# Output projection in four pieces, a third of w_mod moved from VectorE to TensorE, rows spread through DRAM, one multiplication moved to GpSimd

## What is computed

```python
mod_x = silu(c) @ w_mod + b_mod                 # w_mod is 1024 x 6144; six rows of 1024:
x_sh1, x_sc1, x_g1, x_sh2, x_sc2, x_g2 = split(mod_x, 6)
ux = modulate(rmsnorm(x), x_sh1, x_sc1) @ w_in  # the same for the context
pool_x = pool_mixer(ux[:, :512])                # windows 2/4/8/16, then w_pool
ssm_x = ssm_output(scan both ways of ux[:, 512:])  # 32 groups, 64 complex states; then GELU, w_glu
x = x + x_g1 * (concat([pool_x, ssm_x]) @ w_out)
h2 = modulate(rmsnorm(x), x_sh2, x_sc2)
x = x + x_g2 * moe(h2)                          # 32 experts, top 2, each 3 matrices of 2 MB
return rmsnorm(x)
```

## Time and profile before

| | |
|---|---|
| median of 3 runs | 686.17 us (685.89 to 686.75) |
| the profiled execution's own time | 685.61 us |
| its span, first to last instruction | 683.8 us |
| TensorE busy (matmuls) | 596.1 us, 87% |
| VectorE, ScalarE, GpSimd busy | 207.4, 147.6, 35.7 us |
| moved by DMA | 247.27 MB, 362 GB/s over the span |

### The profile page before, as it was taken

How to read it: one execution, slowest core, us unless ns; L and a number is a source line. 1 busy time by engine, 2 the same in 40 slices (tenths; PEclk the granted TensorE clock), 3 DMA queues, 4 the chain that set the end, 5 groups by cost and what they waited for, 6 DMA issues and landing times.

```text
span 683.8 us, 9370 instructions
## 1 busy us (share of the span) xinstructions
PE 596.1 (87%) x3784; PEld 253.1 (37%) x3784; DVE 207.4 (30%) x432; ACT 147.6 (22%) x235; POOL 35.7 (5%) x84
## 2 busy tenths in 40 slices
PE   1878999869878999789889978988997898899995
PEld 0345463446434334234323423422342342234331
DVE  7987979538663002001000200100020010002003
ACT  7163051022112212110301211130121213011111
POOL 4364000000000000000000000000000000000000
PEclk9999999988979999999989999998999999899999
DMA  8992177899866999999999999999999999998951
GB/s 319 417 391 66 30 260 292 302 372 404 335 256 263 424 422 420 422 422 422 422 422 422 421 422 422 422 422 422 422 422 422 422 422 422 422 422 342 422 230 62
DMA packets 45807, 247.27 MB, mean 362 GB/s; under 512 B 8548, under 2 KB 11252, under 8 KB 18520
## 3 DMA queue, kind: packets, MB, share of 16 engines
q1 hardware_dynamic: 41032, 244.45, 87.9%
q10 hardware_dynamic: 4448, 1.57, 0.9%
q0 software_dynamic: 304, 0.93, 0.4%
HBM read 242.75 MB, written 2.10 MB: 358 GB/s over the span
## 4 chain that ended last, share of the span: by engine, by line
PE 64%; DMA 21%; DVE 3%; issue 2%; ACT 2%; SPq 1%; ACTq 0%; POOL 0%; DVEq 0%; POOLq 0%
DMA wts<-in_w_up 21%; PE ps L784 20%; PE ps L819 16%; PE ps L758 5%; PE ps L540 4%; PE ps L752 4%; PE ps L549 2%; PE ps L617 2%; PE ps L666 1%; PE ps L677 1%; PE ps L795 1%; PE ps L463 1%; DVE ra L1070 1%; PE ps L647 1%; PE ps L566 1%
## 5 line engine op out<-in xcount | busy, mean ns | idle before, releaser
L784 PE MATMUL ps<-wts,ra 128*64 128x512 f32 x512 | 240.1, 624 | 37.3 <-DMA wts<-in_w_up 36.1
L785 PE MATMUL ps<-wts,ra 128*64 128x512 f32 x512 | 240.2, 624 | 0.0
L784 PEld LDWEIGHTS ps<-wts,ra 128*64 128x64 f32 x512 | 70.5, 143 | 186.5 <-issue 137.2
L819 PE MATMUL ps<-rc,ra 128*32 128x512 f32 x512 | 111.4, 593 | 0.0
L819 PE MATMUL ps<-wts,ra 128*32 128x512 f32 x512 | 111.4, 593 | 0.0
L1070 DVE TENSOR_TENSOR ra<-ra,ps 128x256 f32<-128x256 f32 x32 | 13.5, 421 | 297.7 <-ACT ra L1023 297.5
L1017 ACT COPY ra<-ps 128x512 f32<-128x512 f32 x32 | 33.6, 1049 | 232.5 <-PE ps L785 232.5
L785 PEld LDWEIGHTS ps<-wts,ra 128*64 128x64 f32 x512 | 70.5, 143 | 0.0
L819 PEld LDWEIGHTS ps<-wts,ra 128*32 128x32 f32 x512 | 29.1, 110 | 73.2 <-issue 73.2
L1070 DVE TENSOR_TENSOR cb<-ps,ra 128x512 f32<-128x512 f32 x32 | 22.1, 692 | 103.4 <-PE ps L819 103.4
L1012 ACT COPY ra<-ps 128x512 f32<-128x512 f32 x32 | 18.5, 588 | 114.5 <-PE ps L752 108.6
(11 more groups left out here) (228 smaller groups left out, 507.4 us busy)
## 6 DMA issues: line engine op xcount, KB each, us to landing
wts<-in_w_up SPq DMA_DIRECT2D x64, 1024.0 KB, 15.3
wts<-in_w_gate SPq DMA_DIRECT2D x64, 1024.0 KB, 13.2
wts<-in_w_down SPq DMA_DIRECT2D x30, 1024.0 KB, 9.4
rc<-in_w_down SPq DMA_DIRECT2D x30, 1024.0 KB, 12.5
wts<-in_w_mod SPq DMA_DIRECT2D x15, 1024.0 KB, 13.1
r<-in_w_mod SPq DMA_DIRECT2D x7, 1024.0 KB, 7.3
wts<-in_w_in SPq DMA_DIRECT2D x2, 2048.0 KB, 23.0
wts<-in_w_out SPq DMA_DIRECT2D x2, 2048.0 KB, 11.6
```

The source lines that it names most:

```text
L784: pe.matmul(ps[0:64, 4 + b, :], st, Wg[b][:, k, :], start=(k == 0), stop=(k == KD - 1))
L785: mm = pe.matmul(ps[64:128, 4 + b, :], st, Wu[b][:, k, :], start=(k == 0), stop=(k == KD - 1))
L819: mm = pe.matmul(ps[32 * j:32 * j + 32, BANKS[n], :], hid[:, j, f, SLOTS * t:SLOTS * t + SLOTS], Wd[j][:, f, 512 * h:512 * h + 512], start ...
```

## The change

- **Last third of w_mod.** `mod_sum` and `acc` are gone. TensorE takes the 8 pieces as it takes the others (4 matmuls each, PSUM bank 7), between pieces of other work. The pieces go to four buffers (`wm2`).
- **Rows through DRAM.** The rows of the bias and of the products stay in `modrow`. ScalarE writes them to the DRAM tensor `row_dram` with a DMA, and `sp` reads each back with a DMA that gives it to all 128 partitions: `gffb` (0.5 MB), `g1b` and `sh2b` (1 MB together), `sc2b` (0.5 MB), `g2b` (0.5 MB). VectorE makes `A2b` of `sc2b` and `gffb` in one instruction. `spread`, lines 684, 690, 734 and 735 and ScalarE's four copies are gone.
- **mix_pool in four pieces** of 4 matmuls, among the pieces of w_mod and the parts of `y` and GLU. The Toeplitz part of `y` comes ahead of them.
- **Toeplitz kernels** go to `wts`, where `ST` was, and their 15 DMAs are issued ahead of the loads of w_mod blocks 6 and 7 and no longer wait for the input projection.
- **Half of the second direction's `MO`** (6 of VectorE's instructions of 128x1024) goes to GpSimd, and VectorE waits for it (`mo_back`) ahead of its scan.
- **Transposes of SA**: those of the first direction's second half come after the last w_mod block of third 0, those of the second direction between the matmuls of `u_ssm(1)`. VectorE copies three of the sets.
- **First loads of the experts**: up of expert 0 and down of expert 1 among the last w_mod blocks; down of expert 0 after `mix_pool`.
- **gather in two halves**: gathers 0 and 1 ahead of `gate_up(i, 0)`, 2 and 3 after its k = 3.

```diff
@@ SyncE
             sp.wait_ge(S("s_mm"), 8)
-            sp.dma_start(wpool, w_pool[0].rearrange("g c d -> c g d")).then_inc(S("wpool_in"), 16)
             sp.dma_start(wo_pool, w_out_v[:, 0:4, :]).then_inc(S("wo_pool_in"), 16)
-            for k in range(6, KD):
-                mod_chunk(1, k)
-
-            sp.wait_ge(S("u_pool_mm"), NT)
-
             sp.wait_ge(S("kt_ready"), 2)
             for t in range(L):
...
+            for k in range(6, KD):
+                mod_chunk(1, k)
+
+            sp.wait_ge(S("u_pool_mm"), NT)
+            sp.dma_start(wpool, w_pool[0].rearrange("g c d -> c g d")).then_inc(S("wpool_in"), 16)
             sp.dma_start(wglu, w_glu[0].rearrange("(k p) n -> p k n", p=P)).then_inc(S("wglu_in"), 16)
             sp.dma_start(wo_ssm, w_out_v[:, 4:8, :]).then_inc(S("wo_ssm_in"), 16)
             for k in range(3):
                 mod_chunk(2, k)
...
-            sp.wait_ge(S("mix_pool"), 1)
+            sp.wait_ge(S("gff_row"), 16)
+            sp.dma_start(gffb, row_dram[1:2, 0:D].broadcast_to([P, D])).then_inc(S("gff_in"), 16)
+            sp.wait_ge(S("mod1_row"), 16)
+            sp.dma_start(ra[:, 6144:8192], row_dram[0:1].broadcast_to([P, 2048])).then_inc(S("g1_in"), 16)
+            sp.wait_ge(S("pool_mm"), 1)
+            mod_chunk(2, 3)
+
             sp.wait_ge(S("hp_ready"), 1)
+            mod_chunk(2, 4)
             sp.wait_ge(S("y_mm"), 1)
             for t in range(NT):
                 sp.dma_start(x2[:, t, :], x[0, t * P:(t + 1) * P]).then_inc(S(f"xres_in{t}"), 16)
+            mod_chunk(2, 5)
             gu_load(sp, 0, 0, 0, "up")
             gu_load(sp, 0, 0, 1, "up")
-            for k in range(6, KD):
-                mod_chunk(2, k)
+            mod_chunk(2, 6)
             for half in range(2):
-                down_load(sp, lambda j: j, half, (0, 1))
-            sp.wait_ge(S("mod2_used"), KD)
+                down_load(sp, lambda j: j, half, (1,))
+            mod_chunk(2, 7)
+            sp.wait_ge(S("mix_pool"), 1)
+            for half in range(2):
+                down_load(sp, lambda j: j, half, (0,))
+            sp.wait_ge(S("mod2_row"), 16)
+            sp.wait_ge(S("hp_ready"), 1)
+            sp.dma_start(sc2b, row_dram[2:3, 0:D].broadcast_to([P, D])).then_inc(S("sc2_in"), 16)
             gu_load(sp, 0, 0, 0, "gate")
@@ GpSimd
+            gp.wait_ge(S("kk_mm"), 2)
+            gp.wait_ge(S("sa_t"), 16)
...
+            for h in range(2):
...
+                gp.tensor_tensor(MOv[:, 1, 0, g], pr, cr, ALU.mult)
+                step(gp.tensor_tensor(t, pi, ci, ALU.mult))
+                step(gp.tensor_tensor(MOv[:, 1, 0, g], MOv[:, 1, 0, g], t, ALU.subtract))
+            gp.sem_inc(S("mo_back"), 1)
@@ TensorE
+            mix_pool(0)
+            for k in range(3):
+                mod_chunk(2, k, 7)
 
             pe.wait_ge(S("hp_ready"), 1)
...
+            for k in range(6, KD):
+                mod_chunk(2, k, 7)
+            mix_pool(3).then_inc(S("mix_pool"), 1)
             pe.wait_ge(S("wo_ssm_in"), 16)
@@ TensorE, gate_up
                     if j == 0 and k == 0:
-                        pe.wait_ge(S("xm_ready"), 4 * i + 3)
-                    if j == 0 and k == 6:
-                        pe.wait_ge(S("xm_ready"), 4 * i + 4)
+                        pe.wait_ge(S("out_copy"), 4 * i + 3)
+                    if j == 0 and k % 2 == 0:
+                        pe.wait_ge(S("xm_ready"), 4 * i + k // 2 + 1)
...
+                    if j == 0 and k == 3:
+                        pe.wait_ge(S("out_copy"), 4 * i + 4)
+                        gather(2)
+                        gather(3)
@@ VectorE
+            dve.wait_ge(S("sc2_in"), 16)
+            dve.wait_ge(S("gff_in"), 16)
+            link(dve.scalar_tensor_tensor(A2b.rearrange("p (k q) -> p k q", k=KD), sc2b.rearrange("p (k q) -> p k q", k=KD), 1.0,
+                                          gffb.rearrange("p (q k) -> p k q", k=KD), ALU.add, ALU.mult))
```

More of the change, by code:

```diff
@@ L160, in hybrid_block @@
         sg = rc[:, 3072:4096].rearrange("p (q t c) -> p q t c", q=4, t=L)
-        g1b = cb[:, 3072:4096]
+        g1b = ra[:, 6144:7168]
+        sh2b = ra[:, 7168:8192]
+        gffb = ra[:, 4096:5120]
+        sc2b = cb[:, 0:1024]
         g2b = ra[:, 6656:7680]
         gfb = r2[:, 0:1024]
-        A2 = aux[:, 16:24]
-        A2b = rc[:, 1024:2048]
-        sh2b = rc[:, 4096:5120]
-        A2diag = rc[:, 2048:3072]
+        A2b = rc[:, 0:1024]
         x2 = rc[:, 6144:8192].rearrange("p (t d) -> p t d", t=NT)
@@ L610, in _ @@
             mm.then_inc(S("pool_mm"), 1)
-            pe.wait_ge(S("wo_pool_in"), 16)
-            pe.wait_ge(S("cat_pool"), 1)
-            for n in range(4):
-                for k in range(4):
-                    mm = pe.matmul(ps[:, n, :], cat[:, k, P * (n // 2):P * (n // 2) + P],
-                                   wo_pool[:, k, 512 * (n % 2):512 * (n % 2) + 512], start=(k == 0), stop=False)
-            mm.then_inc(S("mix_pool"), 1)
             pe.wait_ge(S("toep_in"), 16 * (2 * L - 1))
@@ L651, in _ @@
             mm.then_inc(S("y_mm"), 1)
[L652 to L653 removed]
+            mod_chunk(2, 3, 7)
+            mix_pool(1)
             pe.wait_ge(S("ysb_ready"), 1)
@@ L658, in _ @@
             mm.then_inc(S("y_t"), 1)
+            for k in range(4, 6):
+                mod_chunk(2, k, 7)
+            mix_pool(2)
             pe.wait_ge(S("wglu_in"), 16)
@@ L943, in _ @@
             u_evacuate(0)
+            for n in range(8, 2 * KD):
+                copy_st(n)
             u_evacuate(1)
-            copy_st(1, 0)
-            copy_st(1, 1)
             u_evacuate(2)
@@ L1043, in _ @@
                 four(i)
-                for r in range(4):
+                for r in range(2):
                     take_gathered(4 * i + 4, r)
@@ L1144, in _, with powers_times @@
             dve.sem_inc(S("bbar_ready"), 1)
-            def powers_times(dst, pw, m, d, sign_im, done):
-                    for rr in range(2):
+            def powers_times(dst, pw, m, d, sign_im, done, rs=(0, 1), between=None):
+                    for rr in rs:
+                        if between and rr == 1:
+                            between()
                         for h in range(2):
```

239 lines of the change are left out of this document (108 added, 131 removed).

## The result

The changed kernel takes 698.46 us (median of 4 runs, 697.82 to 700.06), the kernel before 686.03 beside it (681.41 to 686.75). The ratio is 1.0187, with a 95% interval of 1.0157 to 1.0218: **12.4 us slower**. The forecast was slower, by 5.5 us, in a range of 682.5 to 698. The side was right; the size was less than half of what came, and the result lies above the range. The profiled execution has a span of 696.9 us against 683.8.

What follows compares the result with a forecast made beforehand. DMA's expert-weight stream bounds the kernel, so residual delay reaches the end: 7.2 + 1.0 − 0.1 − 0.7 − 1.1 + 1.2 − 1.8 = +5.7 on 685.61 gives 691.3, as median 691.9; stated 691.5 us, range 682.5 to 698.

Steps and rivals of the forecast that it cites:

- What bounds the kernel: Experts' weight stream: DMA is saturated, so one microsecond of delay of VectorE's residual is one microsecond at the end.
- The last block of w_mod: Ahead of the output projection's end: block lands at 168.2, TensorE is there at 162 to 164 and waits about 5 us.
- From the block to the residual: From w_mod's last block through mix_pool(3), down loads, row sc2b and A2b: residual at 182.1 against 174.81, taken as +7.2.
- +7.2: At the residual: its delay in us through the last w_mod block, mix_pool(3), down loads, row sc2b and A2b.
- +1.0 for the clock: TensorE's work after w_mod's last block: a clock lowered by the wait costs 1.0 us, at most 3.4.
- The router and the gathers: Between residual and first gate_up: no A2b wait −0.1, no g2b products −0.7, half the gathers and copies later −1.1.
- The cold clock at the first expert: First half of gate_up may run at half clock, TensorE having less to do before it: +1.2, between 0 and +3.4.
- Later: In the last four experts: half the gathers go behind k = 3, so gu_half comes earlier and the DMA gap closes, −1.8.
- The sign that I had named for it: In the last four experts: DMA share well over 0.08 in the two microseconds around their first gate load.
- GpSimd's share of MO: Ahead of VectorE's scan: GpSimd's six instructions cost nothing, if each stays under 4.35 us.
- Stream in time: Rival, chance 0.22: w_mod's last block lands at 160 to 162, TensorE does not wait; −2.6 in sum, 683.5 us.
- the −1.1: Ahead of the first gate_up: two of four gathers and two of ScalarE's four copies come later, 1.1 us saved.

Runs made afterwards that it cites:

- run 12: Changed kernel with row sc2b and w_mod's last blocks issued earlier, gathers whole, and only one of the 15 Toeplitz DMAs: 683.95 us.
- run 16: Kernel before with only one of its 15 Toeplitz DMAs: 683.21 us, ratio 0.9948 to the kernel before.
- run 14: Changed kernel with row sc2b and w_mod's last blocks earlier, gathers whole, w_out's halves, GLU matrix and gff, g1, sh2 rows issued later: 684.54 us.
- run 15: Changed kernel with three filler matmuls ahead of the router's counts and four more behind gather(1): 697.38 us.
- Runs 5: Kernel before with the gathers in two halves as the only edit: 687.82 us, ratio 1.0031 to the kernel before.
- Run 10: Changed kernel with three filler matmuls ahead of the router's counts only: 700.46 us.
- run 7: Changed kernel with row sc2b and w_mod's last blocks issued earlier and all of MO on VectorE again: 691.66 us.
- runs 2 and 3: Changed kernel with w_mod's last blocks 6 and 7 ahead of first up/down loads: 696.25 us; with also row sc2b ahead of expert 0's down halves: 691.23 us.

## Why the prediction was right in its side and wrong in its size

- **What bounds the kernel** held: one microsecond of the residual was one at the end in all of the runs, to within about 1 us, once the clock of the first `gate_up` is set apart ("rest" is 471.2 to 472.4 in every execution that had it full; from the residual to the first `gate_up` it is 34.9 to 36.0 in the changed kernel and its variants with gathers in halves, 36.1 to 36.9 with whole ones).
- **The last block of w_mod.** Predicted to land at 168.2 with TensorE there at 162 to 164; it landed at 169.8, and TensorE came at 167.2 and waited 2.65. The step behind it was wrong in one half: I took back the queue's idle time and asked only that the Toeplitz DMAs leave no hole. They left none, but they held the engines full at 278 GB/s, a cost that I had put at nothing: 4.7 us at the residual (run 12), where they had cost 2.0 before (run 16). A new hole opened from 144 to 148, where SyncE waits for `y_mm`. And TensorE's wait of 6.45 at 119.54 is not in the prediction at all; behind it the two blocks took 1.93 and 1.94 at the half clock, against 1.04 and 1.07 in run 14, which does not wait. I had looked for a wait at the last block only. TensorE's arrival was 3 to 5 us later than I had it.
- **From the block to the residual.** The order was right: `mix_pool(3)`, SyncE, down, row, `A2b`. From the issue of the down halves to the `A2b` instruction it was 9.2 instead of 7.7, and `A2b` took 2.02 instead of 1.28; unlike L1318 it runs through one operand, `gffb`, in strides, which I take for the reason but did not test. The terms +7.2 and +1.0 for the clock became **+11.2**, mis-sized by 3.0: 1.6 by the landing, 1.5 by the row, 1.0 by `A2b` and the gap behind it, less the 1.0 for a low clock, which this execution did not have at this place.
- **The router and the gathers.** −1.9 predicted, −2.3 measured. Right.
- **The cold clock at the first expert.** The mechanism was right and the term too small: +1.2 predicted from a range of 0 to 3.4; 2.6 came up to the first `gu_half`, and 3.0 at the end (rest 475.4 against 472.4 with filler, run 15). Runs 5, 10 and 15 and the table show it: gathers 2 and 3 had been the work ahead of the first `gate_up`, and without them TensorE stands idle there for 2.4 to 4.2 us. The Trainium skill, page "TensorE: Matmul & The Clock Gate", section "Why this matters for your kernels", warns of gaps between bursts. Run 10 agrees: its clock was full ahead of a gap of 4.15 us and half behind it. I had named it for the blocks of w_mod, where it spoke for the change, and not for the gathers, where it spoke against it.
- **Later.** This is the step that failed: "Half of them go behind k = 3, so `gu_half` is 1.9 earlier, and the gap at 626 to 628 is about that long: −1.8". The program in front of me would have told better: the second half's load waits for the second `gu_half`, and gathers 2 and 3 now stand ahead of that. The sign that I had named for it did come: DMA's share around the first gate load is 0.63 (638 to 640) instead of 0.08. But the loads behind it come later, and DMA thins a second time (0.80 from 644 to 646, 0.91 at 283 GB/s in the next two). In place of −1.8 the runs at full clock show between 0 and +1.2. With the cold first half, the rest grew by 4.2 in place of 1.2 − 1.8 = −0.6. That is 4.8 of the 7.4 missing microseconds, 3.0 of it by this step and 1.8 by the clock if run 15 is taken for both; the residual's 3.0 and −0.4 for the router make up the rest.
- **GpSimd's share of MO**: no cost, as predicted (run 7), 2.85 us each on the mean against 4.35 that would have bound. That VectorE's own products would become slower is not in the prediction; it fell into slack.
- **The rivals.** "Stream in time" named 163 as the landing that decides; the fourteenth run has TensorE at block 7 without a wait at 161.39, and it is level with the kernel before, where that rival had −2.6. This is no full test of the rival, since run 14 has the gathers whole and so neither the −1.1 nor the −1.8; without these two the rival's sum is +0.3, and run 14's span is 683.1 against 683.8.

What stays open: why two of ten executions with gathers in halves had the full clock through the first half (runs 2 and 3, with the same gap of 2.43 ahead of it as the changed kernel), which part of the 4.7 us of the Toeplitz DMAs is their bytes and which their packets, and why `A2b` took 2.02.
